# Output projections begun inside the last heads of GLA and DA, and two slots of the next phase in the tails of out0 and out1

## What is computed

```python
def gla_mixer(x, w_in, w_a2, b_a2, norm_g, w_out):        # layer 1: gated linear attention, 4 heads
    ...
    o = gla_chunked(q, k, v, log_a)
    o = o * lax.rsqrt(jnp.mean(o * o, axis=-1, keepdims=True) + RMS_EPS)
    o = o.reshape(bsz, s, GLA_DV_TOTAL) * norm_g.astype(jnp.float32)
    return (o.astype(x.dtype) * jax.nn.silu(g)) @ w_out

def _diff_attention(h, positions, w_in, ..., subln_g, w_out, lambda_init):   # layer 3, 8 heads
    ...
    o = _rmsnorm(o, subln_g) * (1.0 - lambda_init)
    o = o.reshape(b, s, DA_WIDTH) * jax.nn.silu(z)
    return o @ w_out

x = layer_norm(DEEPNORM_ALPHA * x + y, ln_g[layer], ln_b[layer])     # behind layers 1 and 2
h = _rmsnorm(x, norm_g[i]) * (1.0 + scale) + shift                    # ahead of layers 3 and 4
x = x + gate * y                                                      # behind layers 3 and 4
```

## Time and profile before

| | |
|---|---|
| median of 3 runs | 3019.07 us |
| the profiled execution's own time | 3015.28 us |
| its span, first to last instruction | 3013.5 us |
| PE busy | 2809.1 us, 93% |
| PE weight loads | 2303.8 us, 76% |
| DVE busy | 1501.9 us, 50% |
| ACT busy | 1185.2 us, 39% |
| POOL busy | 951.4 us, 32% |
| DMA | 162.33 MB, mean 54 GB/s |
| mean granted clock of TensorE | 0.967 |

### The profile page before, as it was taken

One profiled execution on the slowest core, in us unless ns is written; L12 is line 12 of the kernel. 1 busy time (PEld: TensorE's weight loads), 2 busy tenths in 40 slices (PEclk: granted clock), 3 DMA queues, 4 the chain that ended last, 5 costly groups with the idle time before them and its releaser, 6 DMA issues. The chain is left out here.

```text
span 3013.5 us, 38793 instructions
## 1 busy us (share of the span) xinstructions
PE 2809.1 (93%) x14702; PEld 2303.8 (76%) x14702; DVE 1501.9 (50%) x1968; ACT 1185.2 (39%) x1974; POOL 951.4 (32%) x490
## 2 busy tenths in 40 slices
PE   7999997899999999978799999999699979999988
PEld 5887785678888888866577778777486768888876
DVE  6765565704544154456455565566642334444343
ACT  4133222424444244524345545555522334444431
POOL 3553452055344533330333333233021340000020
PEclk9999998999999999988899999999899989999999
DMA  4224323111100100031211111011041110000021
GB/s 155 91 77 132 118 70 118 63 49 36 36 28 29 49 29 28 29 120 42 65 36 43 42 29 43 29 43 35 24 144 36 42 42 15 8 15 8 15 84 56
DMA packets 57305, 162.33 MB, mean 54 GB/s; under 512 B 8400, under 2 KB 10064, under 8 KB 57168
## 3 DMA queue, kind: packets, MB, share of 16 engines
q1 hardware_dynamic: 49968, 134.17, 13.9%
q10 hardware_dynamic: 7200, 26.22, 2.7%
HBM read 133.99 MB, written 17.99 MB: 50 GB/s over the span
## 5 line engine op out<-in xcount | busy, mean ns | idle before, releaser
L108 POOL TENSOR_SCALAR w_hi<-w_raw 128x1024 fp32r<-128x1024 f32 x126 | 138.6, 1100 | 1467.7 <-PE pj L134 525.2
L110 POOL TENSOR_TENSOR w_lo<-w_raw,w_hi 128x1024 fp32r<-128x1024 f32 x126 | 309.9, 2459 | 19.3 <-issue 5.6
L1257 PE MATMUL pj<-x_hi,w_hi 128*128 128x512 f32 x688 | 285.2, 415 | 3.0 <-ACT swa_swapped L1388 3.0
L1259 PE MATMUL pj<-x_hi,w_lo 128*128 128x512 f32 x688 | 269.5, 392 | 0.0
L1258 PE MATMUL pj<-x_lo,w_hi 128*128 128x512 f32 x688 | 269.2, 391 | 0.0
L132 PE MATMUL pj<-x_hi,w_hi 128*128 128x512 f32 x544 | 220.0, 404 | 11.5 <-DVE gate_cumsum L550 7.5
L1704 PE MATMUL pj<-x_hi,w_hi 128*128 128x512 f32 x496 | 216.2, 436 | 7.1 <-ACT da_raw L1819 7.1
L134 PE MATMUL pj<-x_hi,w_lo 128*128 128x512 f32 x544 | 213.7, 393 | 0.0
L133 PE MATMUL pj<-x_lo,w_hi 128*128 128x512 f32 x544 | 213.6, 393 | 0.0
L1706 PE MATMUL pj<-x_hi,w_lo 128*128 128x512 f32 x496 | 195.6, 394 | 0.0
L1705 PE MATMUL pj<-x_lo,w_hi 128*128 128x512 f32 x496 | 195.0, 393 | 0.0
(11 more groups left out here) (352 smaller groups left out, 6730.3 us busy)
## 6 DMA issues: line engine op xcount, KB each, us to landing
w_raw<-w_slots SPq DMA_DIRECT2D x158, 512.0 KB, 3.5
o_t<-ada_t ACTq DMA_DIRECT2D x24, 512.0 KB, 3.6
ada_row<-ada_t ACTq DMA_DIRECT2D x24, 512.0 KB, 3.6
x_res<-o_t SPq DMA_DIRECT2D x24, 512.0 KB, 2.7
o_t<-x_res SPq DMA_DIRECT2D x24, 512.0 KB, 6.5
da_swapped<-da_raw SPq DMA_DIRECT2D x64, 128.0 KB, 2.3
o_t<-x_t SPq DMA_DIRECT2D x4, 1024.0 KB, 9.2
o_t<-x_t SPq DMA_DIRECT2D x8, 512.0 KB, 7.4
```

What stands on the lines that cost most here:

```text
L110: nc.gpsimd.tensor_tensor(g.w_lo[:, u, :], g.w_raw[:, u, :], g.w_hi[:, u, :], ALU.subtract)\
L1257: nc.tensor.matmul(proj(half), g.w_hi[:, u, w], g.x_hi[:, k, cols[half]], start=(k == 0), stop=False)
L1259: mm = nc.tensor.matmul(proj(half), g.w_lo[:, u, w], g.x_hi[:, k, cols[half]], start=False, stop=(k == KT - 1))
```

## The change

1. **Two slots in the gate phase.** POOL's split of slot s0 + 3 and SP's load behind it move from the gate phase to the start of GLA's blocks.
2. **out0 begins in GLA's last head.** For k = 0 to 4 (`GLA_EARLY = 5`) ACT makes x_hi of both halves behind its copy of step p = k, DVE makes x_lo behind the last state update, and PE does the products of units (0,0), (0,1), (1,0), (1,1), one group ahead of the sums L401 and four behind. In out0 these four units start at k = 5. As banks 2 and 3 hold (1,0) and (1,1) from the start, the other units of half 0 take turns in banks 0 and 1.
3. **out2 begins in DA's last head.** For k = 0 to 6 ACT makes x_hi at the end of pass n = k, DVE x_lo in the pass after, and PE the products of (0,0) and (0,1): k = 0 to 5 in passes 2 to 7, k = 6 behind the loop. In out2 only k = 7 is left of the two units, and of x_hi and x_lo.
4. **Two slots of the next phase in the tails of out0 and out1.** `next_slot` does slot 1 too. SWA and DA start at slot 2, and the evacuations of slot 1 read row 1 of `g.pj`.
5. **out1's tail.** The third column sum moves from behind unit (1,6) to behind unit (1,7), and `rstd2(0)` behind ACT's last square.
6. **DA's start.** ACT's exponential of the lambda dots, and what DVE makes of it, move behind the first four copies and the low parts.

```diff
@@ gate_phase, SP and POOL; gla_phase, SP and POOL
-            weight_stream(nc, g, block, "gate")(sp)
+            sp.wait_ge(g.raw_free, s0 + 3)
+            sp.dma_start(g.w_raw[:, 0, :], g.w_slots[s0 + 4]).then_inc(g.raw_full[0], 16)
...
-            split_slots(nc, pool, g, "gate")
+            split_slot(nc, pool, g, s0 + 2, 0)
...
+            sp.wait_ge(g.raw_free, s0 + 2)
+            sp.dma_start(g.w_raw[:, 1, :], g.w_slots[s0 + 3]).then_inc(g.raw_full[1], 16)
             weight_stream(nc, g, block, "gla")(sp)
...
+            split_slot(nc, pool, g, s0 + 1, 0)
             with pool.Fori(0, GLA_HEADS) as h:
@@ gla_phase, PE
+            def out_products(k):
+
+                if k == 0:
+                    pe.wait_ge(g.w_ready, s0 + GLA_HEADS * 6 + 2)
+                    pe.wait_ge(m.gate_free, GLA_HEADS * 2 + 2)
+                pe.wait_ge(m.o_lo_ready, k + 1)
+                w = slice(k * P, (k + 1) * P)
+                for n in range(4):
+                    half, slot = divmod(n, 2)
+                    dst, cols = g.pj[:, half, slot * HALF:(slot + 1) * HALF], slice(half * HALF, (half + 1) * HALF)
+                    nc.tensor.matmul(dst, g.w_hi[:, slot, w], g.x_hi[:, k, cols], start=(k == 0), stop=False)
+                    nc.tensor.matmul(dst, g.w_hi[:, slot, w], g.x_lo[:, k, cols], start=False, stop=False)
+                    nc.tensor.matmul(dst, g.w_lo[:, slot, w], g.x_hi[:, k, cols], start=False, stop=False)
...
                     half(1, 0)
+                else:
+                    out_products(0)
                 pe.wait_ge(m.sq_ready, h + 1)
...
+                else:
+                    for k in range(1, GLA_EARLY):
+                        out_products(k)
@@ gla_phase, ACT and DVE
                     rows_behind(p)
+                    if h == GLA_HEADS - 1 and p < GLA_EARLY:
+                        act.wait_ge(m.head_end, GLA_HEADS)
+                        nc.scalar.activation(g.x_hi[:, p, :], g.o_t[:, p, :], ACT.Copy, scale=0.5).then_inc(m.o_hi_ready, 1)
...
+                if h == GLA_HEADS - 1:
+                    for k in range(GLA_EARLY):
+                        dve.wait_ge(m.o_hi_ready, k + 1)
+                        nc.vector.scalar_tensor_tensor(out=g.x_lo[:, k, :], in0=g.o_t[:, k, :], scalar=0.5, in1=g.x_hi[:, k, :],
+                                                       op0=ALU.mult, op1=ALU.subtract).then_inc(m.o_lo_ready, 1)
@@ out_phase
+EARLY = {0: (GLA_EARLY, ((0, 0), (0, 1), (1, 0), (1, 1))), 2: (KT - 1, ((0, 0), (0, 1)))}
+    first, begun = EARLY.get(idx, (0, ()))
...
+        BANK = [0, 1] * KT if (1, 0) in begun else [0, 1, 2, 3] * (KT // 2)
+        if (1, 0) in begun:
+            BANK[KT:] = (2, 3, 0, 1, 0, 1, 2, 3)
...
-                    sp.wait_ge(m.split, half * KT + 2 * i + 2)
+                    if 2 * i + 1 >= first:
+                        sp.wait_ge(m.split, split_of(half, 2 * i + 1))
...
-                if n >= 4:
-                    pe.wait_ge(m.evac, n - 3)
-                for k in range(KT):
+                if LAST_IN_BANK[n] is not None:
+                    pe.wait_ge(m.evac, LAST_IN_BANK[n] + 1)
+                for k in range(first if (half, slot) in begun else 0, KT):
...
-                if slot == 6 and both:
-                    pe.wait_ge(m.acc3_ready, 1)
-                    column_sums(acc[:, 0, :], bank(1)).then_inc(m.ss2_done, 1)
             if both:
+                pe.wait_ge(m.acc3_ready, 1)
+                column_sums(acc[:, 0, :], bank(1)).then_inc(m.ss2_done, 1)
                 first_sum(1)
                 second_sum(1)
-                next_slot(0, range(KT))
+                next_slot(0, range(KT), (0, 1))
...
-                next_slot(1, range(KT))
+                next_slot(1, range(KT), (0, 1))
...
-                next_slot(1, range(KT))
+                if center:
+                    next_slot(0, range(KT), (1,))
+                next_slot(1, range(KT), (0, 1) if center else (0,))
...
                         pass_one(0, k)
-                    if both and n == 14:
-                        rstd2(0)
...
             if both:
+                rstd2(0)
                 pass_two(0, range(3))
@@ da_phase: PE, ACT
+            def out_products(k):
...
+                for slot in range(2):
+                    nc.tensor.matmul(proj(slot), g.w_hi[:, slot, w], g.x_hi[:, k, cols[0]], start=(k == 0), stop=False)
...
                     if not last:
                         piece(h + 1, n, (0, 1))
+                    elif n >= 2:
+                        out_products(n - 2)
...
-            for e in range(2, 2 * L):
-                piece(0, e, range(KT))
+            for e in range(4, 2 * L):
+                piece(0, e, range(KT), e - 3 if e < 6 else None)
...
             heads(pe, head)
+            out_products(HEADS - 2)
             square_sum(HEADS - 1, 1)
...
+            def out_high(k):
+                act.wait_ge(m.final, 2 * k + 2)
+                nc.scalar.activation(g.x_hi[:, k, :], g.o_t[:, k, :], ACT.Copy, scale=0.5).then_inc(m.o_hi_ready, 1)
...
             for e in range(4):
-                take(0, e)
+                take(0, e, e // 2)
+            act.wait_ge(m.dots_ready, 1)
+            nc.scalar.activation(dots[:, :], dots[:, :], ACT.Exp).then_inc(m.exp_ready, 1)
             high(0, 0, 0)
```

106 lines of the change are left out of this document (62 added, 44 removed).

## The result

The changed kernel takes **2972.57 us**, the median of four runs (2963.47 to 2975.01), against 3019.61 beside it: the ratio is 0.9836, 95% interval 0.9817 to 0.9855. Timed again later on another chip it took 2971.86 (five runs), ratio 0.9839. The prediction was 2971, range 2959 to 2993. The profiled execution took 2975.01 us, 7.7 above the 2967.3 that the sum gave for it; a second profiled execution of the same program took 2970.18. So the size of the whole was right to 2 us in the median, and single terms were not.

A forecast was written before the change was run, and what follows sets the result against it. The prediction took PE to bound the kernel, with time to win only where it idles or runs at the lower clock level. Seven terms summed to -48.0: 2967.3 us profiled, 2971 us for the median, range 2959 to 2993.

The forecast's parts named there:

- the rest: From mla_in's first squares to the last column sum of out3: no change predicted, 0 us.
- 1, start of GLA: Start of GLA: second weight split moves behind the barrier, first projection near 37 us; -4.8 us, worst bound -2.5.
- 2: GLA's last head and out0: 60 matmuls moved early fill PE's waits; -14.0 us, bounds -10 and -15.4.
- 3: Tail of out0, start of swa: new slot fills waits, swa begins at slot 2; -9.5 us, bounds -5 and -11.8.
- 7: out2: 42 matmuls leave and PE's waits between low parts go; -11.6 us, bounds -9.7 and -12.5.
- 4, out1's tail: Tail of out1: column sum moves behind the last unit, pass two starts earlier; -1.6 us, bounds -4 and +3.
- 5, start of DA: Start of DA: slots 0 and 1 done, ACT spared the lambda loads' wait; -11.0 us, bounds -7 and -13.
- 6, DA's last head: DA's last head: added products cost +7.7 us, recovering clock gives 3.2 back; +4.5 us, bounds 0 and +9.
- rival (a): Tails and DA's last head: clock stays low, +5 us per tail, 3.2 not won; 2984 us, chance 0.12.
- (b): out0: new PE waits from two banks or late weights, +10 us; 2981 us, chance 0.07.
- (c): DA's start: chain through q and k rotations decides, one more pass and swap, +6 us; 2977 us, chance 0.08.
- (d): DA: DVE's combine meets POOL more often, slower; 3031 us at 30 more meetings, chance 0.05.

## Why the prediction was right, and where it was not

**Bounds and method.** That PE bounds the kernel and that the gain lies where it idles or runs low held. The sum gave -48.0; the medians moved by 47.0, the two profiled executions by 40.3 and 45.1. Of the 3.8 us that I added for the profiled execution of before lying under its median, the changed kernel's own profiled execution has the opposite (2.4 above), so that the closeness of 2971 to 2972.57 is luck by some us. The misses of steps 5 and 6 point the same way and don't cancel, 6.5 and 5.2 us in the two profiles. That the second one comes within 2.9 of the sum is owed to 2.8 us in the rest, where nothing was changed.

**1, start of GLA: right at the entry, partly kept.** The first projection starts at 36.91 ("near 37"). DVE's L576 takes 2.48 us for its two passes beside POOL's split, and 2.48 without it before, and the split takes 2.37: neither held the other up. The Trainium skill (SBUF — State Buffer, Who interferes with whom) states that a DVE instruction with at most one SBUF input, outside the two-port modes, does not contend with GpSimd; the trace agrees. The step at the end of GLA is smaller than the term in most executions (-5.1 to -2.4), by a lower level inside the gate phase or inside GLA.

**2, 3 and 7** were right within 0.9 us each, and 2 and 3 in their mechanism: six low parts of 9.3 us in out0, the late split that swa waits for. They hold in all executions (within 0.4 us for 3, 1.1 for 7). In 7 the number holds better than its working: 42 matmuls (9.7 us) and three waits of 1.1 us make -13.0, not the -11.6 that stands there, and why 1.4 less was taken isn't said. Measured is -11.6 to -12.7.

**4, out1's tail:** -2.9 and -1.7 against -1.6. The marks split it as said: 5.6 and 4.8 us won up to the square sums, 2.7 and 3.1 given back in the second half (the prediction had 4.3 won, and by its total 2.7 given back).

**5, start of DA: the step that failed.** "Slots 0 and 1 are done" and "ACT no longer waits for the lambda vectors" were one term of -11.0, with bounds of -7 and -13, and came to -7.7 and -7.1. The runs part them: the vectors' move is worth 3 to 4 us in the traces (3.4 in the medians), the second slot nothing in the whole (2971.53 without it), since the 3 us that it gives here are paid in term 4. What was missed is that the phase was no longer bound by PE's slots. The chain was in the sum, but two of its links were too short: the swapped halves came 3.9 us after the end of slot 2's split (1444.22 to 1448.11), where the sum had 2.9, and the split of slot 3 took 4.6 us (1455.34 to 1459.93), not 3.5 (the parts 2.9, 7.2 and 3.5 make 13.6, where the sum has 13.9). So slot 3 began 15.8 us after the end of slot 2's split and not 13.9. From there to the scores it took 13.65 us and not 12.3, at a mean clock of 0.87, and they came at 29.4 and not 26.2. That the order of POOL's work was the bound is shown by the kernel with slot 3 split first, whose scores come 3.8 to 5.2 us earlier.

**Why 4.6.** Its pass took 3.39 us, from 1456.54, where DVE's low part of q had begun just before it:

```profile
1456.50 1.22 DVE L1981 SCALAR_TENSOR_TENSOR da_q_lo<-da_raw,da_q_hi 128x1024 fp32r<-128x1024 f32 x1 [10.71 <-ACT da_q_hi L1887]
```

Before the change it was the other way round. POOL's pass came first, then DVE's low part, which took 3.24 us:

```profile
1487.86 2.39 POOL L110 TENSOR_TENSOR w_lo<-w_raw,w_hi 128x1024 fp32r<-128x1024 f32 x1
```

```profile
1488.09 3.24 DVE L1923 SCALAR_TENSOR_TENSOR da_q_lo<-da_raw,da_q_hi 128x1024 fp32r<-128x1024 f32 x1 [14.47 <-ACT da_q_hi L1831]
```

The Trainium skill (SBUF — State Buffer, Who interferes with whom) says that a DVE instruction with two SBUF inputs contends with a GpSimd instruction that reads SBUF, and that the order of issue decides who blocks. Both traces agree. A sum that carries over one engine's duration alone gets the other's wrong.

**6, DA's last head: the mechanism right, one term not there.** The pass takes 7.92 us where nothing disturbs it ("8.0"). But -3.2 for a clock that recovers did not come: at a mean clock of 0.92 against 0.91 before, over a longer stretch, as much is lost as before. In the eight executions with this head its mean clock is 0.88 to 0.95; at half the rate that is an estimated 3.4 to 8.5 us lost, against 5.6 before, so the full credit came in none. So the step costs 5.8 to 7.7 instead of 4.5, near the 7.7 that stood ahead of that credit, and up to 10.4 in other executions (median of the eight 8.0). This is rival (a) at one of its two places; in out0 and its tail the level did follow: over out0 and swa's first slots the changed kernel's PEclk is 0.96:

```profile
477.88:621.12 143.24, 132.60 (x542) 103.62 (x543) 84.80 (x114) 48.18 (x73) 57.41 (x29) 0.96 0.31 109
```

and that of the kernel before, from the same first to the same last instruction, 0.91:

```profile
480.20:648.42 168.22, 152.43 (x602) 118.23 (x603) 89.99 (x124) 53.38 (x83) 59.03 (x29) 0.91 0.27 94
```

**The rivals.** (b) is out (0.5 us). (c) is what happened in part, for another reason than its own: POOL's order, not a rotation more. (d) did not show: the combine takes over 1.5 us in 14 of 64 cases, as many as before.

**What the sum left out:** up to 2.5 us inside swa and 2.1 inside GLA, where no instruction changed, and up to 4.1 won behind mla_in's start. All three go with the time at the lower level. Swa, from its first transposes to its last product, takes 659.9 us before and 660.0 to 661.1 in nine executions, all with 10.2 us of it at the lower level, but 661.5 to 662.4 in the four with 13.7 or 17.1. From mla_in's squares to the end it takes 702.2 to 702.6 in the three executions (before and the first of the changed kernel among them) with 40 us at the lower level, and 698.5 to 701.7 in the eleven with 27 to 34. What makes the level fall at one or another piece of the same work was not found.

## What to carry to other kernels

Work that is moved ahead pays only where the engine that takes it was the bound: ask of each new slot what the phase then waits for (here POOL's order and one ACT copy), and undo the edits one by one, since two that came together can have one effect. Put filler products into waits that exist, not ahead of an instruction whose result another engine takes in a fixed order. And measure before you thin out a stretch of PE that is already sparse: here the idle time next door was worth filling with work from behind it, while filling it with products taken out of the head made the whole 10.7 us longer, for reasons that were only in part taken apart.

## What was not expected of the hardware

- A head with fewer matmuls took longer. In DA's last head 314 matmuls took 61.4 us at a mean granted clock of 0.97, and 273 took 67.7 us at 0.84, where the work removed had stood in short waits. Put the other way: before the change 272 took 61.1 us at 0.91, so the head with 42 products more in its short waits is 0.3 us longer.
- The change took 56 us (199 to 143) off the time at the lower level over the whole run. Only a part of it was spent on matmuls: PE's busy time fell by 10.7 us with the same 14702 matmuls, against 40.3 for the span.
- Steps without any edit differ by 1 to 2.8 us between two executions of one program, and by up to 4.1 over all executions with the same code there, and single runs of the changed kernel lie 11.5 us apart (2963.47 to 2975.01), against 4.4 in the four runs of before beside it (the nine runs of before in later comparisons spread over up to 9.5). One profile of such a kernel is not enough to read terms under 3 us.
